# A two-layer mixture-of-experts decoder: the expert slots become a ring of six, the expert groups are written out, and the gate weights load behind the experts

## The reference

```python
scores = sigmoid(x @ router_w)                 # 256 tokens x 64 experts
choice = scores + router_b                     # best 4 of 8 groups, then best 8 experts
w = scores[chosen] / sum(scores[chosen]) * 2.5
for e in range(64):                            # each token goes to 8 experts
    xs = x[tokens of e]
    h = silu(xs @ w_gate[e]) * (xs @ w_up[e])  # 1024 -> 256
    acc[tokens of e] += (h @ w_down[e]) * w    # 256 -> 1024
y = acc + (silu(x @ s_gate) * (x @ s_up)) @ s_down
```

## Time and profile before

| | us |
|---|---|
| median of 3 runs | 1363.0 (1362.3 to 1363.36) |
| the profiled execution | 1363.32 |
| its span | 1361.5 |
| PE busy in the span | 1333.6 |
| DVE busy | 469.8 |
| ACT busy | 288.7 |
| moved by DMA | 460.65 MB, mean 338 GB/s |

### The profile page before, as it was taken

One profiled execution on the slowest core, in us unless ns is written; L12 is line 12 of the kernel. 1 busy time (PEld: TensorE's weight loads), 2 busy tenths in 40 slices (PEclk: granted clock), 3 DMA queues, 4 the chain that ended last, 5 costly groups with the idle time before them and its releaser, 6 DMA issues.

```text
span 1361.5 us, 18619 instructions
## 1 busy us (share of the span) xinstructions
PE 1333.6 (98%) x6158; PEld 675.2 (50%) x6158; DVE 469.8 (35%) x1310; ACT 288.7 (21%) x516; POOL 14.2 (1%) x20
## 2 busy tenths in 40 slices
PE   7999999999999999998999998999999999999998
PEld 6864544444455444444445554455444444544453
DVE  4745233333323333334312254323333332233342
ACT  1512121112122211212312321122211111222121
POOL 0001000000000000000000010000000000000000
PEclk9998999999999999999999999999999999999999
DMA  9936599999999999988332343999999999999910
GB/s 370 420 145 247 230 424 424 418 417 421 422 423 420 422 419 416 421 344 366 132 146 93 139 186 144 422 419 421 418 417 416 415 419 418 421 420 418 416 52 31
DMA packets 46391, 460.65 MB, mean 338 GB/s; under 512 B 5281, under 2 KB 5538, under 8 KB 7202
## 3 DMA queue, kind: packets, MB, share of 16 engines
q1 hardware_dynamic: 45072, 454.75, 80.6%
q10 hardware_dynamic: 1298, 5.62, 1.1%
HBM read 459.30 MB, written 1.05 MB: 338 GB/s over the span
## 4 chain that ended last, share of the span: by engine, by line
PE 87%; DVE 4%; DVEq 4%; issue 2%; ACT 1%; DMA 1%; SPq 0%; ACTq 0%
PE ps L371 83%; DVEq L1197 3%; PE ps L570 2%; PE ps L448 1%; DVE onehot L1169 1%; PE ps L575 1%; DVE scratch L1210 1%; ACT y_hi L750 1%; DMA lnp<-in_rows 1%; DMA weights<-in_win 0%; DVE scratch L1215 0%; DVE scratch L1112 0%; DVE gtmp L1107 0%; ACT scratch L750 0%; PE ps L689 0%
## 5 line engine op out<-in xcount | busy, mean ns | idle before, releaser
L371 PE MATMUL ps<-weights,scratch 128*64 128x512 f32 (+1 forms) x3232 | 750.4, 596 | 1.9 <-ACT scratch L750 1.9
L371 PEld LDWEIGHTS ps<-weights,scratch 128*64 128x64 f32 (+1 forms) x3232 | 245.6, 140 | 450.0 <-issue 446.4
L750 ACT ACTIVATE scratch<-ps 128x512 f32<-128x512 f32 (+2 forms) x218 | 113.2, 520 | 538.0 <-PE ps L371 531.2
L1226 DVE SCALAR_TENSOR_TENSOR y_lo<-ps,slot_weight,y_hi 128x512 fp32r<-128x512 f32 x128 | 96.1, 751 | 179.7 <-ACT y_hi L750 179.7
L750 ACT ACTIVATE y_hi<-ps,slot_weight 128x512 fp32r<-128x512 f32 x128 | 87.9, 687 | 287.2 <-PE ps L371 287.2
L371 PE MATMUL ps<-weights,xT 128*128 128x512 f32 x320 | 140.2, 593 | 0.0
L371 PE MATMUL ps<-onehot,x_hi 128*128 128x256 f32 x544 | 113.3, 290 | 0.0
L371 PE MATMUL ps<-onehot,x_lo 128*128 128x256 f32 x544 | 109.4, 282 | 0.0
L371 PEld LDWEIGHTS ps<-onehot,x_hi 128*128 128x128 f32 x544 | 86.1, 190 | 29.7 <-issue 27.0
L371 PEld LDWEIGHTS ps<-weights,xT 128*128 128x128 f32 x320 | 59.9, 190 | 70.2 <-issue 70.2
L371 PE MATMUL ps<-y_hi,onehot_T 128*128 128x512 f32 x264 | 91.4, 427 | 3.3 <-DVE y_lo L1226 3.3
(11 more groups left out here) (143 smaller groups left out, 560.6 us busy)
## 6 DMA issues: line engine op xcount, KB each, us to landing
weights<-in_experts SPq DMA_DIRECT2D x128, 2048.0 KB, 9.9
weights<-in_experts SPq DMA_DIRECT2D x128, 1024.0 KB, 8.7
weights<-in_pgate SPq DMA_DIRECT2D x8, 1024.0 KB, 6.0
weights<-in_wkv SPq DMA_DIRECT2D x8, 1024.0 KB, 9.2
weights<-in_win SPq DMA_DIRECT2D x7, 1024.0 KB, 19.0
weights<-in_shared SPq DMA_DIRECT2D x6, 1024.0 KB, 13.2
weights<-in_wout SPq DMA_DIRECT2D x4, 1024.0 KB, 27.5
lnp<-in_rows ACTq DMA_DIRECT2D x4, 1024.0 KB, 6.1
```

The source lines that it names most:

```text
L371: return nc.tensor.matmul(out, lhsT, rhs, start=first, stop=last, skip_group_check=shared_bank)
L750: return nc.scalar.activation(out, in_, f, **kw)
L1226: v.scalar_tensor_tensor(y_lo[:, hs], PS[:, 4 + h, :], wslot[:, 0:1], y_hi[:, hs].bitcast(F32), ALU.mult, ALU.subtract).then_inc(S(f"y_out ...
```

## The change

**Slots.** All 18 units become six expert slots (0 to 5), used in turn: the expert at place p of the order takes slot p mod 6, and its loads are issued when the expert at place p - 6 has been used. Experts 0 to 5 keep their places. The shared expert moves to units 15 to 17, `pg0` to `pg3` to 13 to 16, `ple` to 12; the last five now load when place 59's down weights have been used.

**Order.** The other 58 experts are sorted by their token count. Two more matmuls on PE give the counts as a column, DVE compares every expert with all others, and PE permutes the rank and weight tables with four small float32 matmuls (`mwT`, `place`, `crep`) after two transposes and a copy by ACT. The one-hot matrices of the first two groups come from the unsorted ranks. SP reads the expert's number from `order`.

**Groups written out.** `SIZES = [2] * 30`: thirty groups of two experts with 64 rows each, as straight code with fixed columns and constant waits. The last four experts (places 60 to 63) and any overflow blocks stay in a `Fori`, now of one turn where nothing overflows. Its group code has the register loads as before, with two more columns loaded for each `ohw`. The first group has no scatter. The overflow table is worked out behind groups 1 and 3.

In straight code DVE writes the one-hot matrices with broadcast tensor_tensor instructions: 4 instead of 8 for the gather, and 2 matches and 2 products instead of 4 for `ohw`.

```diff
-TABLE = NE + OVER + 8
-NITER_MIN = NE // 4
+SLOTS = 6
+SIZES = [2] * 30
+GROUPS = len(SIZES)
+TAIL = STARTS[GROUPS]
+NITER_MIN = 1
...
             def expert_loop(L):
-                sp.wait_ge(S("table"), 1 * L + 1)
-                with sp.Fori(1, n) as i:
+                sp.wait_ge(S("mix_mm"), 4 * L + 2 * TC)
+                expert(L, 3)
+                expert(L, 4)
...
+                sp.wait_ge(S("ordered"), L + 1)
+                for p in range(SLOTS, TAIL, 2):
+                    es = [sp.value_load(order[0:1, L, p + s:p + s + 1], min_val=0, max_val=NE - 1) for s in range(2)]
+                    for s in range(2):
+                        sp.wait_ge(S(f"gu_mm_{L}"), IN_GROUP[p + s - SLOTS] + 1)
+                        gate_up(L, (p + s) % SLOTS, chosen(L, es[s]))
+                    for s in range(2):
+                        sp.wait_ge(S(f"down_mm_{L}"), 2 * IN_GROUP[p + s - SLOTS] + 2)
+                        down(L, (p + s) % SLOTS, chosen(L, es[s]))
...
+                sp.wait_ge(S(f"down_mm_{L}"), 2 * IN_GROUP[TAIL - 1] + 2)
+                load(f"ple_{L}", ple_d[L])
+                for i in range(4):
+                    load(f"pg{i}_{L}", pgate_d[L, i])
...
+                pe.wait_ge(S("placed"), L + 1)
+                pe.wait_ge(S("rank_t_out"), L + 1)
+                for j in range(2):
+                    mm(PS[:, 7, j * P:j * P + P], mwT[:, j * P:j * P + P], place, True, True)
+                mm(PS[:, 7, 2 * P:2 * P + NE], crep, place[:, 0:NE], True, True)
+                mm(PS[0:1, 7, 2 * P + NE:3 * P], cst[:, C_CM + 3:C_CM + 4], place[:, 0:NE], True, True
+                   ).then_inc(S("sorted_mm"), 1)
...
+                for g in range(GROUPS):
+                    ps = range(STARTS[g], STARTS[g + 1])
+                    expert_group(g, g // 2, g % 2, [p % SLOTS for p in ps], [32 * (p // SLOTS) + 32 for p in ps], g == 0)
+                    if g == 3:
+                        overflow()
                 pe.wait_ge(S("table"), L + 1)
                 n = pe.value_load(tab[0:1, L, 0, TABLE - 1:TABLE], min_val=NITER_MIN, max_val=NITER_MAX)
                 with pe.Fori(0, n) as i:
...
-                for part in (y_hi, y_lo):
-                    nc.gpsimd.memset(part[:, :].bitcast(F32), 0.0).then_inc(S(f"y_out_{L}"), 1)
-                nc.gpsimd.memset(ohT[:, :].bitcast(F32), 0.0).then_inc(S(f"turned_{L}"), 1)
...
-                for c in range(TC):
-                    ins = v.tensor_copy(wgtt[:, c, 0:NOBLK].rearrange("p (j e) -> p j e", j=NJ),
-                                        w8[:, c, :].unsqueeze(1).broadcast_to([P, NJ, NE]))
-                step(ins)
...
+                def matches(out, ranks, count, rows):
+                    return v.tensor_tensor(out.rearrange("p (s r) -> p s r", s=count),
+                                           iota[:, 0:rows].unsqueeze(1).broadcast_to([P, count, rows]),
+                                           ranks.unsqueeze(2).broadcast_to([P, count, rows]), ALU.is_equal)
...
+                        def weighted():
+                            cols = [column(0, i * 4 + (2 * b + s), NOBLK) for s in range(2)]
+                            ps = [column(1, i * 4 + (2 * b + s), NE - 1) for s in range(2)]
```

More of the change, by code:

```diff
@@ L58 @@
 NOBLK = NJ * NE
-TABLE = NE + OVER + 8
-NITER_MIN = NE // 4
-NITER_MAX = (NE + OVER) // 4
+SLOTS = 6
+SIZES = [2] * 30
+GROUPS = len(SIZES)
+STARTS = [sum(SIZES[:g]) for g in range(GROUPS + 1)]
+TAIL = STARTS[GROUPS]
+IN_GROUP = [g for g in range(GROUPS) for _ in range(SIZES[g])]
+ITERS = GROUPS // 2
+assert TAIL == NE - 4 and GROUPS % 2 == 0 and TAIL % SLOTS == 0
+TABLE = 4 + OVER + 8
+NITER_MIN = 1
+NITER_MAX = 1 + OVER // 4
 AWAY = 1000.0
@@ L290, in _ @@
             sp.dma_start(ptk[:, :, :], pt_d[:, 0]).then_inc(small, 16)
+            for i in range(3):
+                load(f"sh{i}_0", shared_d[0, i])
             sp.wait_ge(S("xb_mm"), KC)
-            expert(0, 0, 0)
+            expert(0, 0)
             sp.wait_ge(S("gate_mm"), KC)
[L294 to L297, removed]
@@ L317, in expert_loop @@
+                        sp.wait_ge(S(f"down_mm_{L}"), freed)
                         for s in range(2):
[L318 to L327, removed]
+                            down(L, 2 * b + s, chosen(L, es[s]))
+                sp.wait_ge(S(f"down_mm_{L}"), 2 * IN_GROUP[TAIL - 1] + 2)
+                load(f"ple_{L}", ple_d[L])
+                for i in range(4):
+                    load(f"pg{i}_{L}", pgate_d[L, i])
+                return n
+            n = expert_loop(0)
@@ L346, in _ @@
             load("sh2_1", shared_d[1, 2])
-            expert(1, 0, 0)
+            expert(1, 0)
             sp.wait_ge(S("q_mm"), TC * 2)
-            expert(1, 1, 1)
+            expert(1, 1)
             sp.wait_ge(S("v_mm"), TC * 2)
[L351 to L358, removed]
+            expert(1, 2)
             expert_loop(1)
@@ new lines, in group_at, with hots @@
+                def group_at(g):
+                    start, size = (STARTS[g], SIZES[g]) if g < GROUPS else (TAIL + 2 * (g - GROUPS), 2)
+                    return start, start + size, size, P // size
+                for g in range(GROUPS):
+                    def hots():
+                        for b in range(2):
+                            lo, hi, size, rows = group_at(g + 2 + b)
+                            for c in range(TC):
+                                ins = matches(oh[:, c, b * P:b * P + P], rankt[:, c, lo:hi], size, rows)
+                        return ins
+                    def weighted():
+                        lo, hi, size, rows = group_at(g)
+                        for c in range(TC):
+                            ins = matches(ohw[:, c, :], rankt[:, c, lo:hi], size, rows)
+                        step(ins)
+                        for c in range(TC):
+                            ins = v.tensor_tensor(ohw[:, c, :].rearrange("p (s r) -> p s r", s=size),
+                                                  ohw[:, c, :].rearrange("p (s r) -> p s r", s=size),
+                                                  wgtt[:, c, lo:hi].unsqueeze(2).broadcast_to([P, size, rows]), ALU.mult)
+                        return ins
+                    expert_group(g, g // 2, g == 0, hots if g % 2 == 0 else None, weighted)
+                    if g == 1:
+                        overflow_blocks()
+                    if g == 3:
+                        overflow_table()
```

420 lines of the change are left out of this document (255 added, 165 removed).

## The result

| | before | after |
|---|---|---|
| median of 20 runs, us | 1362.38 (1360.2 to 1363.37) | 1364.7 (1362.26 to 1367.87) |
| ratio, 95% interval | | 1.002 [1.0013, 1.0028] |
| span of the profiled execution | 1361.5 | 1365.9 |
| DVE busy | 469.8 | 451.0 |
| instruction packets on q8 | 13 | 49 |

What follows compares the result with a forecast made beforehand. PE was taken to bound the kernel, with DMA full too. From the profiled 1363.32 us, -8.3 (even groups), -1.2 (first scatter), +2.4 (ahead of the first group) and +5.2 (tail) sum to -1.9: 1361.4 us, range 1356.5 to 1367.5.

Steps and rivals of the forecast that it cites:

- slower: Outcome that the time rises more than 0.2% (2.7 us) above the median of the kernel before; chance 0.26.
- the tail's term: Group 30: DVE's loop entry and two more register loads delay hh and PE; +2.6 us a layer, 5.2 us.
- Even groups: Groups 2 to 28 in straight code: hh no longer late behind DVE's register work; 8.3 us gone.
- First scatter: First group has no scatter, so its down matmuls start earlier; 0.6 us a layer, 1.2 us gone.
- Ahead of the first group: Before the first group: sorting matmuls, ACT's copy and overflow matmul, less `wgtt` copies; +1.2 us a layer, 2.4 us.
- a rival at 15 in 100: Group 30: PE's wait of about 3 us lowers the clock; +5.0 us, 1366.4 us; chance 0.15.
- Transfers: Weight loads in the loops and at their end cost nothing; attention weights start some 2 us later, with slack.
- About 45 us ahead: With the third pair of slots, expert loads start three groups ahead, about 45 us, where a load takes about 10.
- Fetching: Straight code in the groups needs about 40 instruction packets instead of 13; taken to cost nothing.
- The 0.5 us a packet of the rival: Instruction fetches under full DMA queues stall PE 0.5 us each, 40 packets, 20 us, 1381 us; chance 0.08.
- DMA sets the turn: In the loops DMA at 421 GB/s makes a turn 29.9 us, leaving 3.6 us of gain; 1366 us; chance 0.05.
- the edit does not reach hh: Even groups: DVE's new instructions wait for something later than registers, none of 8.3 us comes; 1370 us; chance 0.05.

Runs made afterwards that it cites:

- Experiment 3: Kernel before with one edit: DVE makes the gather's one-hot matrices in the odd group instead of the even one; 1353.88 us, ratio 0.9934.
- experiment 1: Changed kernel with DVE's register loads for the tail's one-hot matrices moved from group 30 to group 31; 1359.46 us, ratio 0.9972.
- experiment 2: Changed kernel with ten idle matmuls added on PE in group 30, ahead of its wait for hh; 1362.50 us, ratio 0.9997.
- experiment 6: Kernel before with one-hot matrices in the odd group, `wgtt` copies behind the shared expert, attention weights held until the norm's load lands; 1348.91 us, ratio 0.9896.
- experiment 7: Changed kernel with the tail's one-hot matrices in the odd group and attention weights held until the norm's load lands; 1352.58 us, ratio 0.9925.
- experiment 4: Changed kernel with four expert slots instead of six; 1368.23 us, ratio 1.0043.
- experiment 8: Changed kernel with four slots and the weight units of the kernel before, gate weights loading before the loop; 1365.04 us, ratio 1.0017.

## Why the prediction was wrong

The time lies 3.3 us above the forecast, inside the range, but it rose where a small fall was forecast; slower had 26 in 100. The step that failed is the tail's term, which priced PE's wait and not the clock behind it; with it failed two places that had no term, the norm's load and the start.

- **Even groups: right.** -8.3 was said; the table gives -7.3, in which the overflow work that moved in stands with 0.3 us a layer (13.28 against 12.97), so -7.9. Experiment 3 gave 8.8 us from the same cause alone.
- **First scatter: right.** From L617 to the down matmuls it took 1.49 us and takes 1.05: 0.4 a layer, where 0.6 was said.
- **Ahead of the first group: a little too dear.** With the scatter the two terms give +0.6 a layer; layer 1, where the clock fell alike in both kernels (5.40 us for the eight rows), measured +0.1.
- **The tail: the step that failed.** "+2.6 us a layer, 5.2 us" against 8.9 in the trace. The wait itself was right: about 3 us said, 2.72 and 2.01 measured, of which experiment 1 took away all. The working was slightly off: the entry costs 3.43 - 2.77 = 0.7 us over four register loads in layer 0 and 3.08 - 2.77 = 0.3 in layer 1, not 1.4. What was missing from the sum is the clock behind the wait, 2.8 and 1.4 us in the trace and 2.2 us together at the median (experiment 2). I had it as a rival at 15 in 100, since a wait of 2.08 us in 632:636 had left the clock at 1.00. Experiments 1 and 2 show that it happens: without the emptiness the clock stays up in both layers.

  The Trainium skill, page "TensorE: Matmul & The Clock Gate", section "Why this matters for your kernels", asks for no idle gap between bursts of matmuls of about the size that was forecast here. By it this rival would have been the forecast, 1366.4 us. The trace agrees that the clock falls behind such a gap, and it fell behind shorter ones too, 2.72 and 2.01 us. A single row with a wait of 2.08 us was too little to set against it.
- **Transfers: wrong.** "They had slack", I wrote of the attention weights. They have: so much that holding them back cost nothing that shows (experiments 6 and 7). What had none was the small load of `lnp` beside them, 8.50 us in the trace of before. In the changed kernel it took 9.73, with the clock's fall behind it, +2.5 us; why it took longer stays open. This term was not in the sum. "About 45 us ahead" was right for the experts and worth nothing to them (experiment 4).
- **The start: missed.** +1.4 us before any changed instruction of the loops runs, in every trace of the changed kernel and its variants; the cause stays open.
- **Fetching: right.** 36 more packets on q8, and no gap on PE put down to "issue" in the thirty groups. The 0.5 us a packet of the rival stood on no row, and none of it shows. The rivals "DMA sets the turn" and "the edit does not reach hh" fell with the 29.74 us of a turn.

For the trace: -1.9 was forecast. Put +3.7 for the tail, +2.5 and +1.4 for the missed terms, and +1.0 for the thirty groups into it, and take off 1.3 for the shorter stretch at low clock and 1.1 for what the two layers cost less ahead of their first down matmul (+0.1 where +1.2 was said): +4.3, what the table gives. The median lies 3.0 us lower than this execution; over the 20 executions such differences go with the clock.

## What to carry to other kernels

Before rewriting a loop to get rid of register work, look for a place in it where the engine has time: one line that moved four register loads by one group gave 8.8 us, the rewrite a small loss. Price a new wait on TensorE as the wait plus the stretch at half clock behind it, above all where the engine would stand entirely still. Where executions of one kernel spread, look at how far the profiled one lies from the median before taking its terms off the median. And when a kernel waits for a small load behind a phase, ask what large loads are issued in the same microsecond, and hold those back by the small one's semaphore.

## What the runs showed of the hardware

- Waits of PE in group 30 of 2.69 to 2.72 us (layer 0) and 2.00 to 2.01 us (layer 1) were each followed by a stretch at a granted clock of 0.50, in the traces of the changed kernel and of experiments 4 and 8; so were the waits of 3.25 to 4.5 us for the norm. Waits of 1.65 us (scatter behind the experts) and of 1.94 to 2.08 us (the norm) were not. Around 2 us it went both ways.
- The fall of the clock ahead of a loop differs between executions of like programs: the eight matmul rows there took from 3.70 us (clock 1.00) to 6.48 us. A single profile cannot price it. In 20 executions of the changed kernel the mean granted clock went from 0.992 to 0.996 and the time from 1367.9 to 1362.3 us.
- One 1 MiB load of `lnp` took 4.7 us (experiment 6) and 6.0 us (experiment 7) when SP held its burst back, and 8.4 to 10.9 us beside it.
- Entering DVE's loop for the tail, with four register loads, took 3.43 us in layer 0 and 3.08 in layer 1; the four loads alone took 2.77 us in a steady turn of the kernel before.
